# One-hots of the expert scatter: from GpSimd alone to VectorE, ScalarE and GpSimd together

## The reference, cut to what matters

```
def peer(xn, w_q, sub_keys, u_tab, v_tab):
    q = (t @ w_q).reshape(n_tok, PEER_HEADS, 2, PEER_HALF)
    sc = jnp.einsum("thpk,hpnk->thpn", q, sub_keys)
    s_top, i_top = lax.top_k(sc, PEER_TOPK)                      # 16 of 128 keys, twice
    cand = s_top[:, :, 0, :, None] + s_top[:, :, 1, None, :]
    best, pos = lax.top_k(cand.reshape(n_tok, PEER_HEADS, kk), PEER_TOPK)
    idx = take(i_top[...,0] * 128 + i_top[...,1], pos)           # expert = i * 128 + j
    g = jax.nn.softmax(best, axis=-1)
    act = jax.nn.gelu(jnp.einsum("phkd,pd->phk", u_tab[idx], t))
    return jnp.einsum("phk,phkd->pd", g * act, v_tab[idx])
```

## Time and profile before

| | us |
|---|---|
| median of 3 executions | 1896.57 (1894.58 to 1899.35) |
| the profiled execution | 1898.83 |
| its span, first to last instruction | 1897.0 |
| PE busy in the span | 1739.9 (92%) |
| DVE busy | 1229.4 (65%) |
| ACT busy | 869.3 (46%) |
| POOL busy | 264.9 (14%) |
| scatter phase, first to last group's matmuls | 380.3 to 621 |

### The profile page before, as it was taken

How to read it: one execution, slowest core, us unless ns; L and a number is a source line. 1 busy time by engine, 2 the same in 40 slices (tenths; PEclk the granted TensorE clock), 3 DMA queues, 4 the chain that set the end, 5 groups by cost and what they waited for, 6 DMA issues and landing times.

```text
span 1897.0 us, 30957 instructions
## 1 busy us (share of the span) xinstructions
PE 1739.9 (92%) x11238; PEld 1589.2 (84%) x11238; DVE 1229.4 (65%) x2177; ACT 869.3 (46%) x1393; POOL 264.9 (14%) x285
## 2 busy tenths in 40 slices
PE   7999899877777999999999998987899989989997
PEld 7999799877767899999998886776799968879997
DVE  7888599844455555555555666685767675557676
ACT  5667423233333444444444554453444444534443
POOL 0000000099999000000000000000100000000000
PEclk9999899988898999999999999998999989989999
DMA  5556444311222555555555566423555544235553
GB/s 193 190 173 214 170 145 146 122 56 67 67 78 67 182 184 188 187 188 188 187 186 186 193 193 219 153 89 100 160 185 187 188 128 140 89 115 185 188 183 105
DMA packets 81321, 292.41 MB, mean 154 GB/s; under 512 B 9057, under 2 KB 10849, under 8 KB 80865
## 3 DMA queue, kind: packets, MB, share of 16 engines
q1 hardware_dynamic: 79632, 286.00, 46.1%
q10 hardware_dynamic: 1616, 5.45, 0.9%
HBM read 289.31 MB, written 2.10 MB: 154 GB/s over the span
## 4 chain that ended last, share of the span: by engine, by line
PE 84%; issue 9%; DVE 4%; ACT 1%; POOL 1%; DMA 0%; DVEq 0%; ACTq 0%; POOLq 0%
PE ps L962 15%; PE ps L963 15%; PE ps L964 15%; PE ps L981 10%; PE ps L983 9%; PE ps L985 9%; PE ps L1046 4%; PE ps L1069 4%; DVE h_tok L1578 1%; POOL h_tok L589 1%; PE ps L957 1%; PE ps L1127 1%; DVE h_tok L1322 1%; ACT high L633 1%; DVE low L1255 0%
## 5 line engine op out<-in xcount | busy, mean ns | idle before, releaser
L1255 DVE TENSOR_TENSOR low<-raw,high 128x1024 fp32r<-128x1024 f32 (+1 forms) x517 | 622.9, 1211 | 361.0 <-ACT high L633 347.0
L633 ACT ACTIVATE high<-raw 128x1024 fp32r<-128x1024 f32 (+1 forms) x517 | 540.7, 1048 | 514.7 <-PE ps L964 283.0
L962 PE MATMUL ps<-xh,low 128*128 128x256 f32 x2376 | 693.7, 292 | 12.9 <-DVE xl L1276 6.8
L963 PE MATMUL ps<-xl,high 128*128 128x256 f32 x2376 | 684.6, 288 | 0.0
L964 PE MATMUL ps<-xh,high 128*128 128x256 f32 x2376 | 684.0, 288 | 0.0
L962 PEld LDWEIGHTS ps<-xh,low 128*128 128x128 f32 x2376 | 469.4, 198 | 22.3 <-DVE xl L1276 7.6
L963 PEld LDWEIGHTS ps<-xl,high 128*128 128x128 f32 x2376 | 468.8, 197 | 5.9 <-issue 1.7
L964 PEld LDWEIGHTS ps<-xh,high 128*128 128x128 f32 x2376 | 468.2, 197 | 0.0
L589 POOL TENSOR_SCALAR h_tok<-consts,yh,spare 128x128 f32<-128x128 f32 x256 | 243.0, 962 | 159.4 <-ACT yh L767 158.9
L981 PE MATMUL ps<-high,yl 128*128 128x512 f32 x688 | 213.7, 392 | 0.1
L983 PE MATMUL ps<-low,yh 128*128 128x512 f32 x688 | 212.6, 390 | 0.0
(11 more groups left out here) (219 smaller groups left out, 1439.1 us busy)
## 6 DMA issues: line engine op xcount, KB each, us to landing
raw<-in_v_tab SPq DMA_DIRECT2D x128, 512.0 KB, 3.4
raw<-in_u_tab SPq DMA_DIRECT2D x104, 512.0 KB, 3.5
raw<-in_ffn_in SPq DMA_DIRECT2D x88, 512.0 KB, 3.4
raw<-in_w_mix SPq DMA_DIRECT2D x56, 512.0 KB, 4.3
raw<-in_ffn_out SPq DMA_DIRECT2D x44, 512.0 KB, 3.5
arena<-in_u_tab SPq DMA_DIRECT2D x24, 512.0 KB, 3.6
raw<-in_w_query SPq DMA_DIRECT2D x16, 512.0 KB, 5.8
raw<-in_diff_qk SPq DMA_DIRECT2D x16, 512.0 KB, 3.7
```

Source lines behind the costliest of these rows:

```text
L633: a.activation(cols(high, p, 0, n), cols(raw, p, 0, n), ACT.Copy).then_inc(slot_high[p.slot], 1)
L962: pe.matmul(dst, left[1], right[0], start=start, stop=False)
L963: pe.matmul(dst, left[0], right[1], start=False, stop=False)
L1255: v.tensor_tensor(cols(low, p, 0, n), cols(raw, p, 0, n), cols(high, p, 0, n).bitcast(F32), ALU.subtract).then_inc(slot_low[p.slot], 1)
```

## The change

In each group of four tokens the four weighted one-hots, so far all made by POOL, are divided: tokens 0 and 1 go to DVE (the same `tensor_scalar`, behind the compare of that group), token 3 stays on POOL, and token 2 goes to ACT. ACT has no compare, so it takes two activations: Abs(sel_j - iota) gives a distance d, and Relu(weight - weight * d) gives the weight where d is 0 and 0 elsewhere (the weights aren't negative). The second one needs the negated weights of the tokens 2 of each group; ACT makes them once, as a 128x64 copy with scale -1 into `params`. PE waits for three semaphores instead of two. DVE and POOL now start when all four chosen arrays have been copied.

```
+        minus_weight = params[:, 0:GROUPS]
...
             for n in range(GROUPS):                      # POOL
                 if n >= 2:
                     pool.wait_ge(scat_done, n - 1)
-                for u in range(4):
-                    t = 4 * n + u
-                    ins = pool.tensor_scalar(one_hot_w[n % 2][:, u * PARTS:(u + 1) * PARTS], iota, sel_j[:, t:t + 1], weight[:, t:t + 1],
-                                             ALU.is_equal, ALU.mult)
-                ins.then_inc(j_hots_ready, 1)
+                t = 4 * n + 3
+                pool.tensor_scalar(one_hot_w[n % 2][:, 3 * PARTS:4 * PARTS], iota, sel_j[:, t:t + 1], weight[:, t:t + 1],
+                                   ALU.is_equal, ALU.mult).then_inc(pool_hots_ready, 1)
...
+            a.activation(minus_weight, bank(0, 0, SEQ).rearrange("p (n u) -> p n u", u=4)[:, :, 2], ACT.Copy, scale=-1.0
+                         ).then_inc(chosen_ready, 1)
             a.wait_ge(sel_turned, 2)
             a.activation(yh[:, SEQ:], bank(1, 0, SEQ), ACT.Copy).then_inc(chosen_ready, 1)
+            def distances(n):                            # ACT
+                t = 4 * n + 2
+                a.activation(one_hot_w[n % 2][:, 2 * PARTS:3 * PARTS], iota, ACT.Abs, scale=-1.0, bias=sel_j[:, t:t + 1]).then_inc(distance_ready, 1)
+            def act_hots(n):
+                t = 4 * n + 2
+                a.wait_ge(distance_ready, n + 1)
+                a.activation(one_hot_w[n % 2][:, 2 * PARTS:3 * PARTS], one_hot_w[n % 2][:, 2 * PARTS:3 * PARTS], ACT.Relu,
+                             scale=minus_weight[:, n:n + 1], bias=weight[:, t:t + 1]).then_inc(act_hots_ready, 1)
+            distances(0); distances(1); act_hots(0); act_hots(1)
             for n in range(GROUPS):
                 a.wait_ge(scat_done, n + 1)
+                if n + 2 < GROUPS:
+                    distances(n + 2)
                 j_end = first_staged(n)
                 a.activation(weights_of(n, 0, j_end), scattered(n)[:, :, 0:j_end], ACT.Copy).then_inc(w_written, 1)
+                if n + 2 < GROUPS:
+                    act_hots(n + 2)
...
             for n in range(GROUPS):                      # PE
-                pe.wait_ge(i_hots_ready, n + 1)
-                pe.wait_ge(j_hots_ready, n + 1)
+                pe.wait_ge(one_hots_ready, n + 1)
+                pe.wait_ge(act_hots_ready, n + 1)
+                pe.wait_ge(pool_hots_ready, n + 1)
...
-            def i_hots(n):                               # DVE
+            def one_hots(n):
                 v.tensor_tensor(one_hot[n % 2]..., ALU.is_equal)
+                for u in range(2):
+                    t = 4 * n + u
+                    ins = v.tensor_scalar(one_hot_w[n % 2][:, u * PARTS:(u + 1) * PARTS], iota, sel_j[:, t:t + 1], weight[:, t:t + 1],
+                                          ALU.is_equal, ALU.mult)
+                ins.then_inc(one_hots_ready, 1)
```

More of the change, by code:

```diff
@@ L383, in build @@
             sem(n) for n in ("shifted_ready", "exp_ready", "sel_ready", "sel_turned", "chosen_ready"))
-        i_hots_ready, j_hots_ready = sem("i_hots_ready"), sem("j_hots_ready")
+        one_hots_ready, act_hots_ready, pool_hots_ready = (
+            sem(n) for n in ("one_hots_ready", "act_hots_ready", "pool_hots_ready"))
+        distance_ready = sem("distance_ready")
         scat_done, w_written = sem("scat_done"), sem("w_written")
@@ L520, in expert_step @@
                 if j == NKEYS - 2:
-                    sp.wait_ge(j_hots_ready, GROUPS)
+                    sp.wait_ge(one_hots_ready, GROUPS)
+                    sp.wait_ge(pool_hots_ready, GROUPS)
+                    sp.wait_ge(act_hots_ready, GROUPS)
                     sp.dma_start(ffn_params, ffn_params_in).then_inc(ffn_params_loaded, 16)
@@ L580, in _ @@
             inverse_roots(0, 2)
-            pool.wait_ge(chosen_ready, 3)
+            pool.wait_ge(chosen_ready, 4)
             pool.wait_ge(h_kept, 16)
@@ L765, in _ @@
             a.activation(weight, bank(0, 0, SEQ), ACT.Copy).then_inc(chosen_ready, 1)
+            a.activation(minus_weight, bank(0, 0, SEQ).rearrange("p (n u) -> p n u", u=4)[:, :, 2], ACT.Copy, scale=-1.0
+                         ).then_inc(chosen_ready, 1)
             a.wait_ge(sel_turned, 2)
             a.activation(yh[:, SEQ:], bank(1, 0, SEQ), ACT.Copy).then_inc(chosen_ready, 1)
+            a.wait_ge(chosen_ready, 4)
+            a.wait_ge(h_kept, 16)
+            def distances(n):
[6 more added lines that the diff above has]
+                             scale=minus_weight[:, n:n + 1], bias=weight[:, t:t + 1]).then_inc(act_hots_ready, 1)
+            distances(0)
+            distances(1)
+            act_hots(0)
+            act_hots(1)
             for n in range(GROUPS):
                 a.wait_ge(scat_done, n + 1)
+                if n + 2 < GROUPS:
+                    distances(n + 2)
                 j_end = first_staged(n)
                 a.activation(weights_of(n, 0, j_end), scattered(n)[:, :, 0:j_end], ACT.Copy).then_inc(w_written, 1)
+                if n + 2 < GROUPS:
+                    act_hots(n + 2)
                 if n % 2 == 1:
@@ L1569, in _ @@
             take_low(piece_staged(LEAD))
-            v.wait_ge(chosen_ready, 1)
+            v.wait_ge(chosen_ready, 4)
             v.wait_ge(h_kept, 16)
             iota4 = iota.unsqueeze(1).to_broadcast([PARTS, 4, PARTS])
-            def i_hots(n):
+            def one_hots(n):
                 v.tensor_tensor(one_hot[n % 2].rearrange("p (t i) -> p t i", t=4),
                                 sel_i[:, 4 * n:4 * n + 4].unsqueeze(2).to_broadcast([PARTS, 4, PARTS]),
-                                iota4, ALU.is_equal).then_inc(i_hots_ready, 1)
+                                iota4, ALU.is_equal)
+                for u in range(2):
[3 more added lines that the diff above has]
+                ins.then_inc(one_hots_ready, 1)
             def weigh_group(n):
@@ L1592, in weigh_staged @@
                 v.tensor_tensor(staged_part(k, 0, t), staged_part(k, 0, t), staged_bank(k, 0, t), ALU.mult).then_inc(staged_weighed, 1)
-            i_hots(0)
-            i_hots(1)
+            one_hots(0)
+            one_hots(1)
             for n in range(0, GROUPS, 2):
@@ L1599, in _ @@
                     v.wait_ge(scat_done, n + 1)
-                    i_hots(n + 2)
+                    one_hots(n + 2)
                 if n >= 2:
@@ L1604, in _ @@
                     v.wait_ge(scat_done, n + 2)
-                    i_hots(n + 3)
+                    one_hots(n + 3)
                 weigh_group(n)
```

## The result

The changed kernel takes 1802.95 us (median of 4 runs, 1800.12 to 1805.44), the kernel before 1895.57 in the runs beside it: a ratio of 0.951, 95% interval 0.9487 to 0.9533. The prediction was 1829 us with a range down to 1811: the direction was right, the gain of 68 us too small against some 93.

A forecast was written before the change was run, and what follows sets the result against it. The prediction took POOL, never idle in the scatter phase, as the bound. With pairs at 5.44 us instead of 7.61, it summed 65.5 us saved in the phase and 2.2 at its start to 67.7, giving 1829 us, range 1811 to 1862.

The forecast's parts named there:

- rival C: Scatter phase: ACT reloads tables at each alternation, 1998 us, chance 0.04; milder form with two loads, 1882 us, 0.03.
- Rival B: Scatter phase: PE's clock stays low for 26% of the time, 5.99 us a pair, 1846 us; chance 0.09 at full size.
- the sum of a pair: Scatter phase, one pair of groups: mean floor 5.04 us plus 0.4 for DVE and POOL side by side, 5.44 us.
- the 0.4 us for DVE beside POOL: Scatter phase: DVE's new instructions wait for POOL's, 0.2 us twice a pair, bounds 0 and 1.57.
- the floor of 5.04 us: Scatter phase: mean over four quarters of a pair's time, set by PE or DVE, whichever needs more.
- DVE's load: Scatter phase: DVE's 3.61 us a pair plus four new instructions of 0.35 us, 5.01 us a pair.
- PE's floor: Scatter phase: two groups' weight loads of 0.89 us and 2.97 us of `project_in` matmuls, 4.75 us a pair.
- the quarters: Four parts of the scatter phase, DVE's load rising through it, taken at 4.75, 5.0, 5.1 and 5.3 us a pair.
- ACT's load: Scatter phase: ACT's 2.78 us a pair plus 1.82 for two Abs and two Relu, 4.6 us, under DVE's mean.
- PE's idle time small and many times: Sign expected in the changed kernel's scatter phase: PE idles often but briefly, with groups 5.4 us a pair.
- The range's low end: Fast case of the scatter phase: at 4.8 us a pair 154.8 us, time 1809; the range given starts at 1811.
- rival A: Scatter phase: port locked, each POOL instruction stands in full before a DVE one, 6.61 us a pair, 1865 us; chance 0.12.

The follow-up runs named there:

- pelight: Changed kernel with 16 instead of 24 matmuls in each of the 32 staged blocks' products of the scatter phase (low-weights product left out): 1793.9 us.
- dve4: Changed kernel with all four weighted one-hots of a group on VectorE, none on ScalarE or GpSimd: 1825.5 us.
- dve3: Changed kernel with three one-hots of a group on VectorE, one on ScalarE, none on GpSimd: 1810.0 us.
- poolbusy: Changed kernel in which GpSimd makes each of its one-hots twice more, into a buffer that nobody reads: 1858.4 us.
- poolmemset: Changed kernel in which GpSimd zero-fills its one-hots by a memset, leaving token 3 out of the result: 1802.1 us in one run.
- dve2pool2: Changed kernel with two one-hots of a group on VectorE, two on GpSimd, none on ScalarE: 1819.9 us.

## Why the prediction was wrong

What held. POOL was the bound and is none now; the three makers are covered by the double buffers; SP's loads are not late (110 GB/s against the estimate of 100). The single lengths were right: 341 ns for the new DVE instruction (0.35 predicted), 397 and 456 for Abs and Relu (0.41 and 0.50), the first group at 378.4 (378.1), no table load. Against rival C the prediction had the earlier trace rows and a rule of the Trainium skill ("ScalarE: Activation LUTs", section "Table sets: the hidden batching unit": cheap functions are in every set); the trace after agrees, Abs and Relu run between Copy and gelu without a load. Rival B didn't come either: the low level ends at 382.3 us and doesn't return in the phase, as PE's weight loads in the changed kernel show by their length:

```profile
381.92 0.33 PEld L990 LDWEIGHTS ps<-xh,low 128*128 128x128 f32 x1
382.14 0.27 PEld L991 LDWEIGHTS ps<-xl,high 128*128 128x128 f32 x1
382.33 0.19 PEld L992 LDWEIGHTS ps<-xh,high 128*128 128x128 f32 x1
```

**The step that failed is the sum of a pair, 5.44 us; it is 4.67.** Over 30 pairs that is 23.1 of the 27.1 us by which the phase (174.3 predicted, 147.2 measured) was overrated: 12.0 are the 0.4 us for DVE beside POOL, 11.1 the floor of 5.04 us, which made DVE the bound where PE is. Three terms were mis-sized.

- DVE's load, 5.01 us by adding 4 x 0.35 to the busy time. In the changed kernel DVE is busy 143.69 us in 150, that is 32.2 pairs of 4.66 us, so 4.46 a pair; pelight, where DVE sets the pace, gives 4.4. There a DVE instruction with another ready behind it costs its length less 0.08 us. The new ones by that are 4 x 0.26 = 1.04 us a pair, which with the 3.61 of before would be 4.65; the other 0.19 are mostly old instructions that stood alone before and have one ready behind them now (`weigh_staged` in every pair, `take_low` in a third), or are some 20 ns shorter (the compare and `take_low`). The prediction had this as a lower bound (0.28) and then chose the duration because it was "the row of the same opcode". The row was right and the wrong quantity was taken from it: dve4 and dve3 put the cost at 0.26.
- The 0.4 us for DVE beside POOL. It is zero as far as the steps from start to start show: 0.26 us from one new instruction to the next in the changed kernel, and 0.26 in dve3, which has nothing on POOL. The trace of before showed already that POOL is the one that yields; the prediction set that aside because the new instruction has one source. The line of that instruction in the changed kernel has no tail:

```profile
L1612 DVE TENSOR_SCALAR h_tok<-consts,yh,spare x128: 328/342/365, 377.4 to 523.9; 128x128 f32<-128x128 f32 x128
```

- PE's floor, 4.75 us. It is 4.66: the 24 steps of `project_in` take 2.88 us and not 2.97, 0.120 each, since the interval read from the earlier trace rows held the longer first step (0.20 us between the first two matmuls).

With DVE at 4.46 and no term for POOL, the bound is PE in all but the last two pairs, so DVE's uneven load, which made up the quarters, matters only in the last two.

The rest, 4.0 us, is the frame. The first pair took 6.24 us instead of 8.4, since the low clock level ended 4 us after the first group; and the last half pair is one group of 0.89 us, which I had counted as half of 5.44.

The other two makers were misjudged as well, without effect on the time. ACT's load was put at 4.6 us a pair, again by lengths; it was busy 123.10 us in the 32.2 pairs, 3.8 each. POOL's two instructions were put at 1.6 us; at 1.39 each they are 2.8, since each starts 0.06 us into a compare. And the sign "PE's idle time small and many times" didn't show: PE has no gap after its start.

The range's low end, 1811, rested on a fastest pace of 4.8 us, hardly over the 4.75 that PE was given: a phase of 154.8 us and a time of 1809. The phase was 147.2. Of these 7.6 us the pace is 3.9 (30 pairs of 4.67 instead of 4.8) and the frame 3.7, so even the case of PE as the bound, 1808 us by the prediction's own terms, lay outside the range. A small slip of the prediction besides: the bound of POOL's mean twice comes to 1875 us, not 1876.

The Trainium skill's rule on the shared ports (page "SBUF — State Buffer", section "Who interferes with whom": the one that starts second blocks until the other has ended) gave rival A, 1865 us. Here the measurement decides against it as far as DVE goes: its new instruction is at most 0.14 us over its median in poolbusy and its compare 0.18, whoever starts first. For POOL the trace agrees where it starts second: inside a compare or `take_low` it was held until that one had ended. That GpSimd's reads compete with VectorE's second source, which the same section states too, agrees with poolmemset, whose memsets beside those two weren't held up.

## What to carry to other kernels

When an engine is to take over work, add to its busy time the new instructions' spacing from start to start in a full queue (here 0.26 us), not their durations (0.34 here, 0.40 in dve3); the gap is small for one and decides the bound for many. Then ask which engine of the rest is next, and take its floor from the steady spacing of its own instructions: the pace here was simply TensorE's 4.66 us. Work divided over several engines is finished when each is just behind the bound, and more on any one (0.5 us a pair on VectorE, one token on ScalarE, one on GpSimd) costs 7 to 17 us at once. A helper that shares something with another engine is best started while that engine does something harmless: POOL's one-hot, started 0.06 us into a compare, takes 1.39 us instead of 0.79. No run here tried another start.

## What the runs showed of the hardware

GpSimd yields to VectorE, and VectorE hardly to GpSimd. GpSimd's `tensor_scalar` of 0.79 us alone takes 1.39 us in the changed kernel, up to 2.56 in dve2pool2, while a memset mostly keeps its 0.21. What counts is the start: in the kernel before, one that starts inside a VectorE instruction with two sources in SBUF ends 0.58 to 0.68 us after that one, and one that starts over 0.2 us ahead of it keeps its 0.79, whatever VectorE does next. These are lengths read from traces, not the outcome of a run that changed the compare. VectorE's own 128x128 `tensor_scalar` has a median of 341 ns with GpSimd busy 57% of the time (the changed kernel, 380 to 530 us) or all of it (poolbusy), and a longest of 365 and 478.

The granted clock doesn't follow the busy share alone. Before, PE was busy 133.7 us of the 180 from 400 to 580 at a clock of 0.89; in poolbusy it was busy 134.9 of 180 at 1.00. Before, the groups of a pair stood apart, with gaps of over 2 us ahead of the scatter matmuls such as the one at 478.52; in poolbusy they are 1.6 to 1.7, as the timeline of its scatter matmuls shows:

```profile
442.97 1.13 PE L1106 MATMUL ps<-h_tok 128*128 128x128 f32 x8 [1.60 <-DVE h_tok L1620]
...
449.60 1.13 PE L1106 MATMUL ps<-h_tok 128*128 128x128 f32 x8 [1.74 <-POOL h_tok L594]
```

The stretch before, which answers to poolbusy's above:

```profile
400.00:580.00 180.00, 133.73 (x947) 128.98 (x946) 85.96 (x142) 67.58 (x117) 179.93 (x189) 0.89 0.21 68
```

The gaps are not the whole of it either. The busy time at the low clock is longer for the same work: the 133.7 us of before are 947 matmuls, the 134.9 of poolbusy 1104. And later in the phase of the kernel before the clock stayed high through gaps of 2.3 us ahead of the groups at 546, 554, 561 and 568 us, with PE less busy than in the mean:

```profile
540.00:576.00 36.00, 24.37 (x202) 23.57 (x201) 19.46 (x30) 13.78 (x25) 36.00 (x41) 1.00 0.23 73
```

What exactly keeps the clock up wasn't tried.
